# Gate rates of a hybrid diffusion trunk: the small matrix becomes the stationary operand, on four column strips

## The reference

```python
h = modulate(rms_norm(x, lw["norm1_g"]), sh1, sc1)
zq, zk, zv, zqkv, zg, zb, za = jnp.split(h @ lw["w_in"], SPLITS, axis=-1)
...
beta = jax.nn.sigmoid(zb.astype(F32)).reshape(B, T, 2, GDN_HEADS)
g = -jnp.exp(lw["gdn_a_log"].astype(F32)) * jax.nn.softplus(
    za.astype(F32).reshape(B, T, 2, GDN_HEADS) + lw["gdn_dt_bias"].astype(F32))
```

## Time and profile before

| | us |
|---|---|
| three runs, median (lowest to highest) | 1301.71 (1301.47 to 1304.51) |
| profiled execution, first to last instruction | 1298.2 |
| PE busy in it | 1164.0 (90%) |
| DVE busy | 559.1 (43%) |
| ACT busy | 295.0 (23%) |
| mean granted clock of PE | 0.948 |
| DMA moved | 335.43 MB, mean 258 GB/s |

### The profile page before, as it was taken

The page is one execution under the profiler, slowest core; times in us unless marked ns, Lnnn a source line. Parts: engine busy times, 40 slices in busy tenths (PEclk is TensorE's granted clock), DMA queues, the critical chain, the costliest instruction groups (busy, mean ns, idle before and its releaser), DMA issues.

```text
span 1298.2 us, 19389 instructions
## 1 busy us (share of the span) xinstructions
PE 1164.0 (90%) x7971; PEld 572.5 (44%) x7971; DVE 559.1 (43%) x1434; ACT 295.0 (23%) x725; POOL 86.0 (7%) x98
## 2 busy tenths in 40 slices
PE   4999998798999999988779999959889899999874
PEld 1565544375565333322246655436545633333221
DVE  1256886466266111121162678936724721211114
ACT  1237412223131101000021772132312211010000
POOL 0020000210001000000022000021000100000001
PEclk9899999798999999999988999989989999999897
DMA  8560134867946899999955013275574689999994
GB/s 359 171 182 1 66 89 170 241 235 300 405 162 258 311 415 405 413 420 421 411 204 170 1 57 99 81 202 212 191 313 192 226 299 395 421 403 422 420 415 174
DMA packets 95468, 335.43 MB, mean 258 GB/s; under 512 B 34303, under 2 KB 36743, under 8 KB 81031
## 3 DMA queue, kind: packets, MB, share of 16 engines
q1 hardware_dynamic: 88455, 310.66, 62.8%
q0 software_dynamic: 6912, 23.40, 5.1%
HBM read 315.42 MB, written 18.61 MB: 257 GB/s over the span
## 4 chain that ended last, share of the span: by engine, by line
PE 75%; DMA 12%; DVE 5%; SPq 3%; issue 3%; ACT 2%; POOL 0%; ACTq 0%; DVEq 0%
PE bank L537 71%; PE bank L540 4%; DMA ring<-in_moe_w_dram 4%; DMA ring<-in_ada_w_dram 3%; ACT arena L1413 2%; DMA arena<-in_moe_w_dram 2%; SPq L1235 2%; DMA expert_dram<-arena 2%; DVE arena L1727 1%; DMA inv_dram<-ring 1%; DVE x L1735 1%; DVE small L2040 1%; DVE ring L1735 0%; DMA arena<-expert_dram,idx_row 0%; DVE x L1727 0%
## 5 line engine op out<-in xcount | busy, mean ns | idle before, releaser
L537 PE MATMUL bank<-ring,arena 128*32 128x512 f32 (+1 forms) x2560 | 403.8, 594 | 26.0 <-DMA ring<-in_moe_w_dram 8.5
L537 PE MATMUL bank<-arena 128*32 128x512 f32 (+3 forms) x1696 | 316.0, 560 | 23.5 <-issue 11.0
L1413 ACT ACTIVATE arena<-bank 128x512 f32<-128x512 f32 (+3 forms) x308 | 132.1, 475 | 614.8 <-PE bank L540 417.7
L537 PE MATMUL bank<-ring,hT 128*128 128x512 f32 x576 | 254.6, 599 | 2.0 <-DVE hT L1732 2.0
L537 PEld LDWEIGHTS bank<-ring,arena 128*32 128x32 f32 (+1 forms) x2560 | 120.0, 115 | 224.3 <-issue 224.0
L537 PEld LDWEIGHTS bank<-ring,hT 128*128 128x128 f32 x576 | 108.9, 192 | 130.7 <-issue 128.4
L537 PEld LDWEIGHTS bank<-arena 128*32 128x32 f32 (+2 forms) x1696 | 93.4, 123 | 116.3 <-issue 93.2
L1727 DVE TENSOR_TENSOR arena<-bank,mrow 128x512 f32<-128x512 f32 x40 | 27.6, 691 | 254.5 <-PE bank L537 254.5
L537 PE MATMUL bank<-hT,ring 128*128 128x384 f32 x384 | 131.4, 498 | 0.0
L537 PEld LDWEIGHTS bank<-hT,ring 128*128 128x128 f32 x384 | 73.2, 195 | 48.0 <-issue 3.4
L540 PE MATMUL bank<-const,arena 128*128 128x128 f32 x459 | 69.4, 289 | 26.9 <-DVE arena L1727 17.1
(11 more groups left out here) (150 smaller groups left out, 868.4 us busy)
## 6 DMA issues: line engine op xcount, KB each, us to landing
ring<-in_moe_w_dram SPq DMA_DIRECT2D x62, 2048.0 KB, 16.7
arena<-in_moe_w_dram SPq DMA_DIRECT2D x34, 2048.0 KB, 16.1
ring<-in_ada_w_dram SPq DMA_DIRECT2D x24, 2048.0 KB, 8.7
ring<-in_w_in_dram SPq DMA_DIRECT2D x14, 2048.0 KB, 9.9
expert_dram<-arena SPq DMA_DIRECT2D x18, 512.0 KB, 15.8
ring<-in_w_out_dram SPq DMA_DIRECT2D x4, 2048.0 KB, 8.2
arena<-in_na_rpb_dram SPq DMA_DIRECT2D x32, 96.0 KB, 5.3
tok_dram<-arena POOLq DMA_DIRECT2D x6, 512.0 KB, 2.9
```

What stands on the lines that cost most here:

```text
L537: return nc.tensor.matmul(out, lhsT, rhs, start=start, stop=stop)
L1413: return nc.scalar.activation(out, in_, func, **kw)
```

## The change

The gate rates' product is turned round. The small matrix becomes the stationary operand (128 features x 16 columns) and all 384 tokens move, so that eight products do instead of 24. Product `k` goes to column strip `k % 4`, which writes partitions `32 * (k % 4)` to `+ 16` of one bank; chunks `k` and `k + 4` are added up in PSUM. The bank then holds four partial sums, transposed: rates on the partitions, tokens along the row. DVE copies it, 128x384, to `ba_part` in SBUF, in a place of `arena` that nothing else uses at the time. Behind convolution slice 0, `ba_sums()` makes three further products, one for each token tile: 128 tokens of `ba_part` are stationary and a constant 0/1 matrix `pick_ba` of 16 columns moves, which adds the four strips and turns the result back to tokens on the partitions. From there on all is as before. The table of constants grows by 16 columns.

```diff
+    parts["pick_ba"] = t[:, None] % STRIP == np.arange(BA)[None, :]
...
+        ba_part = take(TOK, 13312)
...
                 pe.wait_ge(gates_in, 16 * N_FIRST)
-                b = dve_bank("ba", l)
-                for t in range(TILES):
-                    for k in range(KC):
-                        last = mm(b[:, t * BA:(t + 1) * BA], hT[:, k, t * P:(t + 1) * P], w_ba[:, l, k, :],
-                                  k == 0, k == KC - 1)
+                b = dve_bank("ba_part", l)
+                for k in range(KC):
+                    s = STRIP * (k % QUAD)
+                    last = mm(b[s:s + BA, 0:TOK], w_ba[:, l, k, :], hT[:, k, :], k < QUAD, k >= QUAD)
                 last.then_inc(for_dve, 1)
+
+                def ba_sums():
+
+                    pe.wait_ge(dve_emptied, job["ba_part", l])
+                    b = dve_bank("ba", l)
+                    for t in range(TILES):
+                        last = mm(b[:, t * BA:(t + 1) * BA], ba_part[:, t * P:(t + 1) * P], tab("pick_ba"))
+                    last.then_inc(for_dve, 1)
...
                     last.then_inc(for_act, 1)
                     slab_job[slab] = ("act", jobs["act"])
+                    if f == 0:
+                        ba_sums()
                     if 5 <= f < 11:
                         decay_sums(f - 5)
...
+                b = filled("ba_part", l)
+                vec.tensor_copy(ba_part, b[:, 0:TOK]).then_inc(dve_emptied, 1)
                 b = filled("ba", l)
                 vec.tensor_copy(ba, b[:, 0:48].rearrange("p (t n) -> p t n", t=TILES)).then_inc(dve_emptied, 1)
```

## The result

| | before | changed |
|---|---|---|
| median of 6 runs each (lowest to highest), us | 1300.94 (1297.99 to 1304.51) | 1287.97 (1285.43 to 1292.06) |
| span of the profiled execution, us | 1298.2 | 1285.4 |
| ratio, 95% interval | | 0.9904 (0.9886 to 0.9922) |

The ratio is 12.5 us of 1300.94 (10.1 to 14.8). The prediction had 12.5 us and a time of 1289.2; the measured median is 1.2 us lower, 0.8 of it because the kernel before has a median of 1300.94 in these six runs and had 1301.71 in the three that the prediction started from.

The account below looks back on a forecast made before the run. PE was taken as the bound (busy 90%, 75% of the chain). Product and sums 6.4, clock 5.1 and wait 1.0 sum to 12.5 us: 1301.7 - 12.5 = 1289.2 us, with 8 in 10 for 1284 to 1297.

Parts of the forecast that it names:

- The product and the sums: Gate rates' product and sums behind slice 0: 5.3 - 1.42 - 0.67 = 3.2 us gained a layer, 6.4 in all.
- The estimate from 60 cycles a matmul: Strip product: instruction overhead, if on top, adds 0.4 us a layer, taking 0.8 us from the gain.
- The clock: Narrow product and slice 0: half-clock stretches vanish, 1.7 us in layer 0 and 3.4 in layer 1, 5.1 together.
- The wait: PE ahead of slice 4's gate sums, layer 0: the wait goes as `gates()` ends ahead of POOL, 1.0 us.
- The predicted worst case: Layer 0's `convolve(2)` and `convolve(3)`: DVE stands for all 7.0 us of POOL's work; 1.5 us of loss at most.
- Passing through: From layer 0 to the end: all 12.5 us passed on; layer 1 and the experts' stream start 5.9 us earlier.
- A: Strip product: 16-column strips run one behind the other; gain 5.1 us, time 1296.6; 7%.
- B: Around slice 0: the clock falls all the same; gain 6.4 + 1.0 us, time 1294.3; 12%.
- C: DMA- or POOL-bound stretch gives a gain back, such as layer 0's 5.9 us in the experts' stream; time 1295.1; 10%.
- D: Strip product: strips run serially and halve the clock; 5.6 us more a layer, 11 in all, time 1313; 3%.

Follow-up runs that it names:

- cut-up product: Kernel before, its 24 narrow products split by token tile, each piece behind that tile's `zg` products; ratio 0.9939, 7.9 us less.
- repeated sums: Changed kernel with its three selection products behind slice 0 made eight times over; ratio 1.0008, local 31.54 and 31.50 us.
- third execution: Changed kernel unaltered, run a third time, beside the kernel before on the same chip; ratio 0.9902 (0.9881 to 0.9922).

## Why the prediction was right

**The product and the sums.** Predicted 5.3 - 1.42 - 0.67 = 3.2 us a layer; measured 5.27 - 1.41 - 0.58 = 3.28. The choice that carried it, taking the 32-column strips as the model for 16-column ones, is borne out: 1.41 us against 1.30 of scaled strips and 0.12 for the switch. The sums were put 0.09 us too high, since the group that priced them stood behind a wait (0.89 us for eight; 0.81 in the changed kernel, without a wait). A cost of about the same size was left out: slices 0 to 2 take 15.68 us around the sums (64.26 to 80.52 less 0.58) and 15.57 where they run unbroken behind the old product in pieces (68.85 to 84.42). The estimate from 60 cycles a matmul would have had 0.4 us more a layer; the 1.41 us leave no room for it.

**The clock.** Predicted 1.7 and 3.4 us; the cut-up product shows it alone (3.37 in layer 1), and the repeated sums bring it back (3.4). The local 6.51 us in layer 1 are 3.28 of work, less the 0.11 around the sums, and 3.3 for the clock.

**The wait.** Predicted 1.0 us in layer 0; it is gone, and the cause (POOL beside small DVE instructions) was shown by moving POOL alone. It was worth 1.2: from the transposes ahead of it to the gate sums PE takes 1.51 us with the wait and 0.33 without, while the profile marks 1.02 as idle. So layer 0 has 3.28 - 0.11 + 1.7 + 1.2 = 6.1 us (6.05 measured, 5.9 predicted). `gates()` began at 81.34 (predicted 81.6) and was done before POOL began at 84.29. The predicted worst case came almost whole: DVE's instructions beside POOL took 6.5 us longer (4.51, 1.76 and 3.96 for 2.60, 0.68 and 0.42) of the 7.0 feared. `convolve(2)` ended at 87.5 and `convolve(3)` at 95.7 (at worst 89.8 and 95.8), PE wanted them at 92.39 and 98.74, and no wait of PE followed. Not foreseen: in layer 1 the first instruction of `gates()` now meets POOL (1.88 us at 704.64); `gates()` was done at 707.5, 2.1 us before the gate sums at 709.63.

**Passing through.** Layer 1 began 5.9 us earlier in the profiled execution of the changed kernel (657.87 against 663.81), as predicted. In between the shift went from 6.5 (delta rule) over 6.9 (output products) to 5.6 (experts); the routing's clock accounts for 1 us of that. Hitting 5.9 was luck. The prediction named layer 1's tokens coming less than 5 us earlier as a sign of its being wrong, and in the third execution they came 2.1 us earlier (661.75), with the same 23.49 and 23.48 us locally and the same ratio of 0.9902 over six runs. So that sign was badly chosen: between executions of one kernel the figure moves by more than the 0.9 us that it leaves. The totals decide, and they bear the step out to within 2 to 3 us. That the experts' stream ends earlier by what it starts earlier was argued, and no run shows it more closely than that.

**Rivals.** A (strips in a row) has the wrong premise; its price of 5.11 us for 16 matmuls on one strip measured 5.27. B (the clock falls all the same) is refuted by clock 1.00 in all windows; with the sums four times over the dip came back once, behind 2.59 us of narrow work. C, all of layer 0's gain lost, is excluded by the run with layer 0 alone. D wanted over 0.4 us for a strip matmul; it took 1.41 / 16 = 0.09.

**A misreading** without effect: of the slices 14 to 20 of the DMA row, the first stands at 8 tenths, not 9.

No version was shown to beat the changed kernel. Router logits, 24 narrow products a layer as well, might be treated in the same way; that wasn't tried.

## What to carry to other kernels

A product of a wide matrix with a few columns, with the wide one stationary, costs by its weight loads (PEld was busy for all of its 5.27 us here): make the few columns stationary, let the tokens move, and spread the contraction over four column strips; the extra selection product costs 0.58 us here and wants a covered place. Without the strips, turning it round saves only what the clock gives back, less the sums (3.5 us of 12.6 here). Look at the granted clock behind every stretch of narrow matmuls, not only at the stretch: 5.1 of the 12.6 us gained here lay there, and cutting the stretch up between wide work got them, and with the vanished wait 6.2 us, with no change in the arithmetic.

## What the runs showed of the hardware

- PE's clock fell from 2.4 to 1.2 GHz while the profile showed PE busy all the time, with narrow matmuls: behind 3.95, 4.5 and 5.27 us of them, within the first 3.89 in layer 1 of the run with layer 0 alone (0.94 over these), and once behind 2.59; it did not fall behind pieces of 1.70, nor the other time behind 2.59. PE's busy time is modelled, so it doesn't tell how long the array itself worked in each 0.11 us. Through 5.27 us of matmuls with 16 stationary and 384 moving columns it stayed at 1.00. The Trainium skill ("TensorE: Matmul & The Clock Gate", HAM oscillation — how this bites in real kernels) tells of waits between groups of matmuls as what brings the clock down; here the trace shows no wait.
- 16 f32 matmuls of 384 moving columns with 16 stationary ones take 1.41 us on four strips and 5.27 on one.
- A 24-column DVE instruction of 0.18 us took 3.96 (88.03 to 91.99) beside POOL's two DMA issues and its instruction of 2.95 us (89.00 to 91.95), and 0.18 again once POOL's work was elsewhere.
